# Two mixers in one kernel: order of the last convolution taps, of the channel mean, of a small product and of a head's PSUM banks

## The reference

```
xm = rmsnorm(x) @ w_in                    # 2048 channels
xconv = silu(conv3x3(xm))                 # depthwise
q = xconv @ w_q ; k = xconv @ w_k ; v = xm    # 4 heads of 512
gates = q @ wq_g + k @ wk_g + v @ wv_g
h = mLSTM recurrence, forwards and backwards (q, k, v, gates)
y = (sigmoid(o) * norm(h) + skip * xconv) * silu(z) @ w_out
```

```
p = x @ w_in
log_f = log_sigmoid(p[forget columns] + forget_b)      # 8 heads
cum = cumsum(log_f)
logits = q.k / 8 + cum[t] - cum[s], causal ; probs = softmax ; y_c = probs @ v
h = causal depthwise conv, 31 taps, of (a * sigmoid(b)) ; y_d = silu(layer_norm(h))
mix = concat(y_c, y_d) @ w_out
```

## Time and profile before

| | us |
|---|---|
| median of three runs | 1232.13 (1232.0 to 1232.33) |
| profiled execution, its own time | 1231.82 |
| its span, first to last instruction | 1229.7 |
| TensorE busy | 1184.5 (96%) |
| VectorE busy | 859.3 (70%) |
| ScalarE busy | 615.6 (50%) |
| GpSimd busy | 145.8 (12%) |

### The profile page before, as it was taken

One profiled execution on the slowest core, in us unless ns is written; L12 is line 12 of the kernel. 1 busy time (PEld: TensorE's weight loads), 2 busy tenths in 40 slices (PEclk: granted clock), 3 DMA queues, 4 the chain that ended last, 5 costly groups with the idle time before them and its releaser, 6 DMA issues.

```text
span 1229.7 us, 22923 instructions
## 1 busy us (share of the span) xinstructions
PE 1184.5 (96%) x9270; PEld 1102.6 (90%) x9270; DVE 859.3 (70%) x1440; ACT 615.6 (50%) x1001; POOL 145.8 (12%) x115
## 2 busy tenths in 40 slices
PE   6999999999999999999999899999999989999996
PEld 3777888888888999999999899999889978999996
DVE  5695874468789767655489687664589767866644
ACT  4432654466564455652453544453466755445433
POOL 0000000000000000003002323210008730222000
PEclk9999999999999999999999999999999999999998
DMA  9846312333222355442543445445433233555540
GB/s 387 352 184 270 141 69 70 114 126 138 103 103 104 138 194 202 169 134 77 198 172 138 172 172 197 178 180 198 146 129 136 71 106 135 192 185 178 199 172 35
DMA packets 28900, 195.59 MB, mean 159 GB/s; under 512 B 3464, under 2 KB 3728, under 8 KB 6416
## 3 DMA queue, kind: packets, MB, share of 16 engines
q1 hardware_dynamic: 27776, 191.90, 42.8%
q10 hardware_dynamic: 1040, 2.50, 0.6%
HBM read 193.33 MB, written 1.05 MB: 158 GB/s over the span
## 4 chain that ended last, share of the span: by engine, by line
PE 86%; DVE 6%; ACT 4%; DMA 2%; issue 1%; POOL 1%; SPq 0%; ACTq 0%; DVEq 0%
PE ps L488 25%; PE ps L489 24%; PE ps L490 24%; PE ps L838 2%; PE ps L513 2%; DMA ada_room<-in_weights 1%; PE ps L531 1%; DVE w_lo L1742 1%; PE ps L825 1%; PE ps L660 1%; ACT x_hi L1443 1%; DVE w_lo L1745 1%; DMA ring<-in_weights 1%; PE ps L1056 1%; PE ps L881 1%
## 5 line engine op out<-in xcount | busy, mean ns | idle before, releaser
L1140 ACT ACTIVATE w_hi<-ring 128x1024 fp32r<-128x1024 f32 x284 | 294.9, 1055 | 294.8 <-PE ps L490 207.7
L1745 DVE TENSOR_TENSOR w_lo<-ring,w_hi 128x1024 fp32r<-128x1024 f32 x266 | 328.4, 1253 | 154.0 <-ACT w_hi L1140 147.6
L488 PE MATMUL ps<-x_hi,w_hi 128*128 128x258 f32 (+1 forms) x1216 | 346.4, 285 | 7.6 <-DVE x_lo L2120 4.1
L489 PE MATMUL ps<-x_lo,w_hi 128*128 128x258 f32 (+1 forms) x1216 | 344.2, 283 | 0.0
L490 PE MATMUL ps<-x_hi,w_lo 128*128 128x258 f32 (+1 forms) x1216 | 343.9, 283 | 0.0
L488 PEld LDWEIGHTS ps<-x_hi,w_hi 128*128 128x128 f32 x1216 | 231.0, 190 | 11.0 <-issue 10.8
L489 PEld LDWEIGHTS ps<-x_lo,w_hi 128*128 128x128 f32 x1216 | 231.3, 190 | 0.1
L490 PEld LDWEIGHTS ps<-x_hi,w_lo 128*128 128x128 f32 x1216 | 230.9, 190 | 0.0
L488 PE MATMUL ps<-g_hi,w_hi 128*128 128x256 f32 x608 | 171.9, 283 | 3.6 <-DVE zf L2244 1.2
L489 PE MATMUL ps<-g_lo,w_hi 128*128 128x256 f32 x608 | 170.8, 281 | 0.0
L490 PE MATMUL ps<-g_hi,w_lo 128*128 128x256 f32 x608 | 170.7, 281 | 0.0
(11 more groups left out here) (372 smaller groups left out, 1939.5 us busy)
## 6 DMA issues: line engine op xcount, KB each, us to landing
ring<-in_weights SPq DMA_DIRECT2D x148, 1024.0 KB, 4.9
o_sb<-in_weights SPq DMA_DIRECT2D x10, 1024.0 KB, 7.4
ada_room<-in_weights SPq DMA_DIRECT2D x10, 1024.0 KB, 8.7
ring<-in_weights SPq DMA_DIRECT2D x8, 512.0 KB, 4.1
ring<-in_weights SPq DMA_DIRECT2D x8, 448.0 KB
V<-in_weights SPq DMA_DIRECT2D x3, 1024.0 KB, 24.7
dft<-in_dft ACTq DMA_DIRECT2D x1, 1026.0 KB, 6.6
X<-in_x SPq DMA_DIRECT2D x1, 1024.0 KB, 5.1
```

What stands on the lines that cost most here:

```text
L488: mm(dst, w_h, x_h, start=start, stop=False, skip_group_check=True)
L489: mm(dst, w_h, x_l, start=False, stop=False, skip_group_check=True)
L1140: do(w_hi[:, q % 2, part], ring[:, q % RING, part], ACT.Copy).then_inc(S("hi_ready"), 1)
L1745: v.tensor_tensor(w_lo[:, q % 2, part], ring[:, q % RING, part], w_hi[:, q % 2, part], ALU.subtract).then_inc(S("lo_ready"), 1)
```

## The change

Four edits.

1. **Head 0.** The query weights' blocks go to banks 0, 3, 1, 2 in head 0 (`TQ_FIRST`), each waits for the `xm` tile of its own bank, and `late_turn` comes behind `turn_weights(0)`. The key block in bank 3 waits for two moved query blocks instead of one. `convolve` can be cut: taps 2, 6, 8 and the two closing operations of the last pair come behind the copy of head 0's scores.
2. **Forget product.** Its eight matmuls use four groups of 32 output columns (two each) and give four partial sums. ScalarE copies them into `logit`, and a ninth matmul in front of input slot 4 adds them (`fold_forgets`, a 128 x 8 sum of unit matrices that VectorE makes with three small additions) into bank 5.
3. **Taps.** All of row 2's remaining taps and its final one come ahead of `split_attention(0)`. The wait for GpSimd comes behind the maximum of head 7; row 3's taps follow in three portions. Half of the second output slot's remainder, `split_attention(2)` and the other half come ahead of the wait for the mean.
4. **Mean.** The mean of the convolution comes behind the second half of `mixed_slot(0)`.

```diff
+TQ_FIRST, TQ_BANKS, TK_BANKS = (0, 3, 1, 2), (3, 0, 1, 2), (6, 4, 5, 3)
...
-            late_turn()
...
-                            pe.wait_ge(S("xm_moved"), KE if e == 0 else KE - HC + e)
+                            pe.wait_ge(S("xm_moved"), KE - HC + banks[e] + 1)
                         elif e == 3:
-                            pe.wait_ge(S("queries_turned_moved"), 4 * hd + 1)
+                            pe.wait_ge(S("queries_turned_moved"), 4 * hd + 1 if hd else 2)
...
                 turn_weights(hd)
+                if hd == 0:
+                    late_turn()
...
-                for k in range(KD):
-                    last = mm(ps[0:FH, 4, 0:SEQ], forget_w[:, k, :], X[:, k, :], start=(k == 0),
-                              stop=(k == KD - 1))
+                for j in range(2):
+                    for g in range(4):
+                        k = 4 * j + g
+                        last = mm(ps[32 * g:32 * g + 32, 4, 0:SEQ], vcol("forget_w", FH * k, 32), X[:, k, :],
+                                  start=(j == 0), stop=(j == 1), skip_group_check=True)
                 last.then_inc(S("forget_done"), 1)
+
+            def fold_forget():
+                pe.wait_ge(S("forget_moved"), 1)
+                mm(ps[0:FH, 5, 0:SEQ], fold_forgets[:, :], logit[:, 0, 0, :], start=True, stop=True)\
+                    .then_inc(S("forget_done"), 1)
...
                 if t == 3:
                     forget()
+                if t == 4:
+                    fold_forget()
...
-                        pe.wait_ge(S("probT_moved"), 7)
-                        column_sum(conv_mean, ones_h[:, :], lambda k: acc31[:, k, :], KH, S("norm_in"),
-                                   S("norm_mean"), since("in", "conv"))
...
             mixed_slot(0)
+            pe.wait_ge(S("probT_moved"), 7)
+            column_sum(conv_mean, ones_h[:, :], lambda k: acc31[:, k, :], KH, S("norm_in"),
+                       S("norm_mean"), since("in", "conv"))
...
+                if t == 3:
+                    act.wait_ge(S("forget_done"), 1)
+                    do(logit[:, 0, 0, :], ps[:, 4, 0:SEQ], ACT.Copy).then_inc(S("forget_moved"), 1)
...
-                    convolve(KE - 2)
+                    convolve(KE - 2, taps=(1, 7, 3, 5, 0), last=False)
...
                               ps[:, 4:6, :].rearrange("p b (t j) -> p (b t) j", t=2)).then_inc(S("scores_moved"), 1)
+                if hd == 0:
+                    convolve(KE - 2, first=False, taps=(2, 6, 8))
...
+            def fourth(k0, k1):
+
+                for k in range(k0, k1):
+                    chain.join()
+                    taps(k, (3,))
...
-            dve.wait_ge(S("forget_done"), 1)
-            v.tensor_scalar(frow[:, 0, :], ps[0:FH, 4, 0:SEQ], rows[0:FH, 4:5], None, ALU.add)\
+            dve.wait_ge(S("forget_done"), 2)
+            v.tensor_scalar(frow[:, 0, :], ps[0:FH, 5, 0:SEQ], rows[0:FH, 4:5], None, ALU.add)\
...
             lo(STARTS["odout"])
+            third(25, TAPS - 1)
+            chain.join()
+            final_tap(2)
             split_attention(0)
             maximum(7)
-            third(25, 26)
+            dve.wait_ge(S("pool_order"), 2 * POOL_TAPS - 1)
+            fourth(POOL_TAPS, POOL_TAPS + 2)
             sum_inverse(7)
-            third(26, 27)
+            fourth(POOL_TAPS + 2, POOL_TAPS + 6)
             split_attention(1)
-            dve.wait_ge(S("pool_order"), 2 * POOL_TAPS - 1)
-            for k in range(POOL_TAPS, TAPS - 1):
-                if k == POOL_TAPS + 3:
-                    chain.join()
-                    final_tap(2)
-                if k > POOL_TAPS + 3:
-                    chain.join()
-                taps(k, (3,))
-                if k < POOL_TAPS + 3:
-                    taps(k + 27 - POOL_TAPS, (2,))
+            fourth(POOL_TAPS + 6, TAPS - 1)
             chain.join()
             final_tap(3)
+            lo(STARTS["odout"] + 1, halves=(0,))
+            split_attention(2)
+            lo(STARTS["odout"] + 1, halves=(1,))
             dve.wait_ge(S("norm_mean"), since("mean", "conv") + 1)
             for k in range(KH):
                 v.tensor_tensor(acc31[:, k, :], acc31[:, k, :], conv_mean, ALU.subtract)\
                     .then_inc(S("norm_centred"), 1)
-            lo(STARTS["odout"] + 1)
-            split_attention(2)
```

More of the change, by code:

```diff
@@ L324, in program @@
         shift_of = sc("shift_of", (P, 4, 2))
+        fold_forgets = sc("fold_forgets", (P, FH))
         second.close()
@@ L637, in _ @@
                     ada_rows(N_ADA0 + a)
-            late_turn()
             def turn_weights(hd):
                 q0 = STARTS["qk"] + 2 * hd
-                for part, banks, done in ((0, TQ_BANKS, "queries_turned"), (1, TK_BANKS, "keys_turned")):
+                for part, banks, done in ((0, TQ_BANKS if hd else TQ_FIRST, "queries_turned"), (1, TK_BANKS, "keys_turned")):
                     pe.wait_ge(loaded[part], ((q0 + part) // RING + 1) * 16)
@@ L1260, in _ @@
                     act.wait_ge(S("queries_turned"), 4 * hd + e + 1)
-                    do(V[:, HC * hd + e, :], ps[:, TQ_BANKS[e], :], ACT.Copy).then_inc(S("queries_turned_moved"), 1)
+                    do(V[:, HC * hd + e, :], ps[:, (TQ_BANKS if hd else TQ_FIRST)[e], :], ACT.Copy)\
+                        .then_inc(S("queries_turned_moved"), 1)
                 for e in range(HC):
@@ L1298, in _, with softplus_of_minus @@
                         .then_inc(S("v_moved"), 1)
-            def softplus_of_minus(x, t, ready, done):
-                act.wait_ge(ready, 1)
+            def softplus_of_minus(x, t, ready, done, count=1):
+                act.wait_ge(ready, count)
                 chain.step(do(t, x, ACT.Abs))
@@ L1594, in _ @@
                 if t == 3:
-                    softplus_of_minus(frow[:, 0, :], frow[:, 1, :], S("forget_moved"), S("forget_log"))
+                    softplus_of_minus(frow[:, 0, :], frow[:, 1, :], S("forget_moved"), S("forget_log"), 2)
                 if t == 5:
@@ L1837, in _, with convolve @@
                                                ALU.add, ALU.subtract).then_inc(S("h_ready"), 1)
-            def convolve(c):
+            def convolve(c, first=True, taps=(1, 7, 3, 5, 0, 2, 6, 8), last=True):
                 tap = lambda b, n: vcol("conv_w", (c + b) * 9 + n)
@@ L1846, in convolve @@
                                      for s in (src, dst)]
-                for b in range(2):
+                if not first:
+                    chain.join()
+                for b in range(2 if first else 0):
                     dve.wait_ge(S("xm_moved"), c + (b + 1))
                     chain.step(v.tensor_scalar(dst[b], src[b], tap(b, 4), vcol("conv_b", c + b), ALU.mult, ALU.add))
-                for n in (1, 7, 3, 5, 0, 2, 6, 8):
+                for n in taps:
                     dy, dx = n // 3 - 1, n % 3 - 1
@@ L1861, in convolve @@
                                                               ALU.mult, ALU.add))
-                chain.join()
-                for b in range(2):
+                if last:
+                    chain.join()
+                for b in range(2 if last else 0):
                     o = dst[b][:, 0:CTX - 1]
@@ L2384, in _ @@
             chain.step(v.memset(frow[:, 4, :], 1.0))
+            chain.step(v.tensor_tensor(fold_forgets[:, :], ident[:, 0:FH], ident[:, 32:32 + FH], ALU.add))
+            for g in (2, 3):
+                chain.join()
+                chain.step(v.tensor_tensor(fold_forgets[:, :], fold_forgets[:, :], ident[:, 32 * g:32 * g + FH], ALU.add))
             rest_of_shift(2, vcol("mix_b1", 0, KD))
```

2 lines of the change are left out of this document (removed).

## The result

The changed kernel takes 1224.86 us (median of 4 runs, 1223.07 to 1226.05), the kernel before 1232.23 beside it (4 runs, 1232.0 to 1232.71). The ratio is 0.9933, with a 95% interval of 0.9920 to 0.9946: 8.3 us off, 6.6 to 9.9 by the interval. The two medians are 7.4 apart. The forecast was 1223.8, 8.3 off. That ratio and forecast agree to the tenth is luck, since either measure of the gain is uncertain by more than a microsecond. The profiled execution took 1226.05, 2.0 more than its span. It was the slowest of the four, so positions in it are compared through intervals between two landmarks. In the code after, `triple` is L489 to L491, the column sum L514, the turns L660, VectorE's row taps L2420 and final tap L2447.

The account below looks back on a forecast made before the run. TensorE bounds the kernel, busy 1184.5 of 1229.7 us, so removing its work or stalls counts. 2.2 + 1.2 + 4.9 = 8.3 us off gives 1223.8 us on the median, range 1221.8 to 1227.8.

Parts of the forecast that it names:

- Part A: First mLSTM head: 0.6 us from the query-weight turn plus 1.6 from the scores copy, 2.2 us off.
- The first stall's 0.6: Head 0, TensorE's wait before the late turn: turning query weights first fills or ends part of it, 0.6 us taken.
- Part B: Forget product: 2.05 us off TensorE, of which 1.2 us arrives (ends 0.4 and 1.9).
- The terms on TensorE: Forget product: eight grouped matmuls take 0.91 us and the folding matmul 0.65, against 3.62 before.
- The stall of 0.7 for the transfer: Before the logits: TensorE, 2 us early, waits about 0.7 us for the transfer of the cumulated gates.
- the transfer moves by the same 1.2 as slot 6: Input projection: slot 6 is rounded 1.2 us earlier; its remainder, the scan and the gates' transfer move with it.
- the prediction's sign for this slot: Input projection: slot 6 waiting for its remainder would show the forecast wrong.
- Part C: End of the odd mixer: slot 1's second half 5.5 us earlier, less 0.55 at the first slot: 4.9 us off.
- Clock: Rival, odd mixer's end: the tensor clock falls around slot 1's new stall, costing 1.5 us: 1225.3; chance 0.19.
- rival 2: GpSimd locked out 4.5 us longer as VectorE's hole closes; fourth-row taps 3.3 us later, C 1.6: 1227.1; chance 0.19.
- A second hold of 10 us: Rival, odd mixer: GpSimd held twice, the second like the 10.25 us one: 1235.3; chance of slower 0.03.
- groups that do not overlap: Rival, forget product: B becomes -0.65 and more wait elsewhere: 1225.7; chance 0.04 together with other partial losses still faster.

Follow-up runs that it names:

- e1: The kernel before with the head 0 edit alone (banks, late turn, cut convolution): 1229.96 us, ratio 0.9983.
- w2: The changed kernel with filler matmuls in three norms and the start, and half of output slot 2's rounding behind the root: 1221.64 us, ratio 0.9904.
- p17: The changed kernel with filler matmuls in three norms and 17 convolution taps on GpSimd instead of 18: 1220.92 us, ratio 0.9899.
- e2: The kernel before with the forget product edit alone (four column groups): 1231.96 us, ratio 0.9996.
- e3: The kernel before with the tap and mean edits together, at the end of the odd mixer: 1227.05 us, ratio 0.9957.
- w0: The kernel before with filler matmuls, results unused, in TensorE's waits at three norms: 1230.37 us, ratio 0.9980.
- p19: The changed kernel with filler matmuls in three norms and 19 convolution taps on GpSimd instead of 18: 1221.39 us, ratio 0.9902.
- w1: The changed kernel with filler matmuls, results unused, in TensorE's waits at three norms: 1220.66 us, ratio 0.9904.

## Why the prediction was right, point by point

**Part A, 2.2 forecast, 2.1 in e1.** From the first query product on, the edit gave 1.8, where 1.6 was taken for the scores copy; where the other 0.2 comes from wasn't looked at. The first stall's 0.6 is 0.71 when both kernels are measured from the same release, the move of the last tile. In after's profile it did not show: ScalarE waited 9.63 us for the weights of a slot where it had waited 8.56, so the move came 1.37 later (135.04 against 133.67), and from the last modulation rows to the queries it took 139.65 - 132.26 = 7.39 against 138.99 - 131.88 = 7.11. That is a late transfer. Seven profiles with the new order took 5.78 (e1 and w2), 6.15 (p17), 6.58, 6.60, 7.32 and 7.39, on average 6.5; the four with the old order at full clock took 6.70 to 7.25, on average 7.05. So about 0.5 is left of the 0.6 on average. Why the transfer varies wasn't tested.

**Part B, 1.2 forecast, 1.55.** The terms on TensorE held: 1.07 and 0.60 for 0.91 and 0.65, so 1.9 us went where 2.05 were forecast. The softplus came 1.3 us earlier against the forget product (926.09 - 913.98 = 12.11, before 926.54 - 913.11 = 13.43), as forecast, and so did slot 6's remainder. (The softplus now waits for VectorE's bias, 1.15 us, and no longer for the diagonals.) The stall of 0.7 for the transfer did not come. The step that failed is that the transfer moves by the same 1.2 as slot 6. The remainder of slot 6 itself got shorter, 2.50 us where it took 2.91, and the taps behind it by 0.1: the transfer's issue moved from 940.12 to 939.22, which is 1.77 earlier against the forget product, while TensorE arrived 1.56 earlier. TensorE in turn stood for 0.2 us at the start of slot 6, at 933.11 (0.33 us behind the matmul before it, where 0.12 is usual): ScalarE's move of slot 4's tile, which stands behind its rounding of slot 6, ended at 932.97. (The profile names no releaser; the code has the wait.) That is the prediction's sign for this slot in a small form, for a move and not for the remainder. e2's trace has the same 28.80 us and the same gap, at 931.41.

**Part C, 4.9 forecast, 5.3 in e3.** The times of after are moved by 0.25 us here, so that its first output slot starts at 978.95 as in the rows: final tap 984.93 + 0.48 + 0.25 = 985.66 (forecast 985.65), centring 989.00 (988.9), root 992.79 (992.85), second half of slot 1 995.92 (996.15). The wait in front of that half is 1.16, not 2.0: TensorE was done with the first half at 994.76, 0.6 later than forecast, and the second half could start 0.2 earlier. Given back at the slot's start are 0.55 in e3 and 0.47 in after. Of the 5.7 us up to slot 1's second half, 5.3 are left at the feed-forward's sum, so 4.8 net in after and in e3. What the working did not price: it says that the clock loss at 990 to 994 goes, but not that 1.6 us of the gain are that loss, which w0's profile shows to be no fixed part of the old order.

**Rivals.** Clock: it did not fall in slot 1 in any profile with part C; it fell behind a norm at 690 in after's, for the same wait that before passed at full clock. The right mechanism at the wrong place, and it cost the profiled run 1.9 us. GpSimd: it was in time, but only by 0.04 us, where the prediction gave it about 1. The 2 us of slack without part B were right (1.87 in e3). B took 1.83 of them and not 0.8, because rival 2 came true in part: as VectorE's hole before slot 6's remainder shrank from 0.94 to 0.14 us, GpSimd's multiply behind the first one took 2.94 us, where before it took 0.93, so three pairs of multiply and addition fit in ahead of the gates' sum and not four, and one more stood behind the long hold. e2, with the forget product alone, has the same 2.94. Against the forget product the tap starts 1.63 us earlier than in e3, and GpSimd ends 0.20 later (63.67 us against 63.47). That this just fitted is luck: p19 shows that some 1.9 us more on GpSimd turns into a wait of 1.70. A second hold of 10 us and groups that do not overlap did not occur.

## What to carry to other kernels

Measure an edit between the event that releases a stretch and its first product, not between two absolute times: a transfer or a clock that varies by 1.5 us hides a gain of 0.7. Before crediting an edit with a stretch at half clock, look whether the old kernel always has that stretch. Slack on an engine that is held by another has to be taken again after each edit ahead of it: here one edit took 1.8 us of 1.9. Filling the tensor engine's sparse waits with products whose results nobody reads can give half of what a whole reordering gives: 37 products in three norms gave 4 us on the kernel after, though only 2.5 on the kernel before.

## What was not expected of the hardware

The granted clock is not a fixed property of a program. Executions of the kernel before spread from 1228.9 to 1235.4 us. The fastest of its first series (1228.87) ran at a mean granted clock of 0.995, the slowest (1235.27) at 0.989. An estimate from these: 0.006 of 1230 us is 7 us of clock, about the 6.4 between them. Over its 49 executions in the three series the two go together only loosely. Which waits are followed by a stretch at 0.50 differs from one profile to the next: the norm at 690 in after's and e1's, not in before's, e2's and e3's. Such a stretch is mostly 1.7 us of clock, and 0.7 to 1.9 us of time in the traces of after and w1.

GpSimd is held while VectorE runs taps and remainders back to back. It stood for 10.26 us at one multiply in after, as in the earlier trace rows, from the gates' sum on, as there:

```profile
931.23 2.94 POOL L1730 TENSOR_SCALAR gated<-pad_a,vec 128x256 f32<-128x256 f32 x1
...
939.02 10.26 POOL L1730 TENSOR_SCALAR gated<-pad_a,vec 128x256 f32<-128x256 f32 x1
```

Most of the 17 such multiplies take 0.92 to 1.10 us; four others take 1.35, 1.90, 2.94 and 2.98. The long one ends at 949.28, while VectorE is at its reductions out of PSUM (from 948.40), as it did before at 950.17 (reductions from 949.31). The Trainium skill, GPSIMD Engine Reference, section 1 (Specifications), states the contention with VectorE's instructions of two SBUF inputs; by that rule the trace agrees, and the length of the hold is this trace's own.
